# Half-width products in the inverse of a chunked recurrence

## The chip, the cores and the metric

The kernel runs on one core of a Trainium2 chip. The metric is the device time of one execution in microseconds (us), and shorter is better. The engines are called PE (matrix products; PEld is its weight load), VectorE (DVE in the rows), ScalarE (ACT), GpSimd (POOL) and SyncE (SP).

## The reference

One layer of a hybrid decoder for 2048 tokens of width 1024, in float32. After a norm, one projection feeds two groups: differential attention, and the RWKV-7 recurrence of 8 heads of width 64. Their outputs go through an output projection; a mixture of 32 experts and a gated per-layer embedding follow. What matters here is the recurrence:

```python
def step(state, inp):
    r_t, w_t, k_t, v_t, a_t, b_t = inp
    sa = jnp.einsum('bhvk,bhk->bhv', state, a_t)
    state = (state * w_t[:, :, None, :] + sa[..., None] * b_t[:, :, None, :]
             + v_t[..., None] * k_t[:, :, None, :])
    y = jnp.einsum('bhvk,bhk->bhv', state, r_t)
    return state, y
```

## The kernel before

The kernel is a row of phases, one after the other with a barrier between them: constants, projection, attention, the recurrence (`phase_rwkv`), output projection, routing, experts and the final gate. All the work in question is in `phase_rwkv`.

The recurrence is computed in chunks of 64 tokens (`CK`). A tile has 128 tokens, so two chunks (`CHUNKS`: partitions 0 to 63 and 64 to 127), and there are 16 tiles. Within a chunk the step-by-step update needs the inverse of a triangular 64 by 64 matrix for each head. It is built up by doubling. `T` holds the inverse of the diagonal blocks found so far. Level 0 fills `T` directly from the product `G3`. Each level l from 1 to 5 then does this, for 8 heads and 2 chunks:

- `Tr(l-1)`: four transposes of `T` on PE; ScalarE copies them to `TP` (128x512).
- `X(l)a` and `X(l)b`: products of `AR1` with `T`, one job for each chunk. ScalarE copies each to `X` (128x256).
- `TX(l)a` and `TX(l)b`: products of `TP` with `X`, one job for the even heads and one for the odd. VectorE copies each into `T` by `copy_predicated` under the mask `lv` of the level (`fill_T`, 128x256).

At level l the mask of an entry is set where row and column lie in neighbouring blocks of 2^l, the row's block being the odd one. So only columns in the first half of each block pair of 2^(l+1) can be set: 32 of the 64.

All products here are of float32. The program's `nc.tensor.matmul` appears in the trace as two weight loads and two matmuls, so a job of X or TX, which has 8 products, counts 16 matmuls; with 20 such jobs a tile that makes 320. Weights are 64x64, and the moving operand has 64 columns. A 64x64 weight takes a quarter of the array. An X job reads one half of the partitions and writes both halves, so it alternates between two quarters; so does a TX job.

The engines take their work in fixed orders written out by hand (`PE_JOBS`, `ACT_EV`, `DVE_EV`, `POOL_EV`), each with one counting semaphore. A PE job waits at its start, never in its middle. Between the steps of a level stands other work: after `X1` the job `Wa`, after `TX1` `Wb`; after `X2` `MN0` and `MN1` (L1618 to L1620), and nothing between `TX2b` and `Tr2`; after `X3` `S0`, `RT0` and `RT1` (L1624), after `TX3` `Y0` (L1628, L1630), `S1`, `Ya` and `Yb`; after `X4` `pc` (L1573), after `TX4` `T0` (L1647); after `X5` `T1` and `D` (L1642), after `TX5` `T2` and `T3`, then `Tr5`, and `cum`, `G3`, `G1`, `G2` of the next tile. W, MN, S, RT, Y0 and Y belong to the tile before ("tail"); cum, pc and T0 to T3 prepare the next one ("prep"). Tile 0 has no tail work and the last tile has no prep. PE's program is unrolled over the tiles; the other engines run a loop.

The waits on which the steps of a level hang:

```python
job(f"Tr{level}", make, (DV, "G3b" if level == 0 else f"TX{level}b", 0))
...
     (DV, "G1b" if level == 1 else f"TX{level - 1}b", 0))
...
job(f"TX{level}{f}", make, (AC, f"X{level}b", 0), (AC, f"Tr{level - 1}", 0))
```

Of the kernel before, what the change touches and what calls it, by code (L numbers as in the profile page):

```python
# [14 lines left out]
P = 128  # L15
# [985 lines left out]
HV = 8  # L1001
CK = 64
# [46 lines left out]
def bank_of(name):  # L1049
    return MAIN_JOBS.index(name) % BANKS if name in MAIN_JOBS else BANKS + PREP_JOBS.index(name) % 2  # L1050
# [11 lines left out]
def phase_rwkv(nc, t, ident):  # L1062
# [5 lines left out]
    with ExitStack() as ctx:  # L1068
        sb = lambda n, s, d=F32: ctx.enter_context(nc.sbuf_tensor(n, s, d))
        sem = lambda n: t["semctx"].enter_context(nc.semaphore(n))  # L1070
        two = lambda n, s, d=F32: [sb(f"{n}{k}", s, d) for k in range(2)]
# [10 lines left out]
        pc = two("c_pc", [P, 4, 2])  # L1082
        AR1 = two("c_AR1", [P, HV, 2, CK]); AR2 = two("c_AR2", [P, HV, 2, CK])
        T = two("c_T", [P, HV, CK])
        TT = two("c_TT", [P, HV, CK]); TP = sb("c_TP", [P, 4, 2, CK]); X = sb("c_X", [P, 2, 4, CK])
        WU = sb("c_WU", [P, HV, 2, DH]); RpT = sb("c_RpT", [P, 4, P]); Y0 = sb("c_Y0", [P, RW])
        MT = sb("c_MT", [P, 2, 4, DH]); NN = sb("c_NN", [P, 2, 4, DH]); St = sb("c_Stmp", [P, 4, DH])
        S = [two(f"c_S{k}", [P, 4, DH]) for k in range(2)]
# [3 lines left out]
        lv = sb("c_levels", [P, len(LEVELS), CK], I32); bits = sb("c_bits", [P, 3, CK], I32)  # L1092
# [8 lines left out]
        def bank(name):  # L1101

            return ps[:, bank_of(name), :]
# [6 lines left out]
        def steps(eng, body):  # L1110

            body(-1, 1, {"prep"}, None)
            body(0, 0, {"main", "prep"}, None)
            with eng.Fori(0, (TILES - 2) // 2) as j:
                body(j * 2 + 1, 1, {"main", "tail", "prep"}, j)
                body(j * 2 + 2, 0, {"main", "tail", "prep"}, j)
            body(TILES - 1, 1, {"main", "tail"}, None)
            body(TILES, 0, {"tail"}, None)
# [5 lines left out]
        def group(name):  # L1124
            return "tail" if name in TAIL else "prep" if name in PREP else "main"

        def heads(ap):
            return ap.rearrange("p (h d) -> p h d", d=DH)

        @block.sync  # L1130
        def _(sp):
# [172 lines left out]
        @block.scalar  # L1304
        def _(act):
            act.wait_ge(cs_p, 1)

            def step(i, s, what, j):
                n = 1 - s

                def ev(name, make, *waits):
                    if group(name) in what:
                        for e, other in waits:
                            act.wait_ge(e.sem, e.value(other, i))
                        AC.in_order(name)
                        make().then_inc(AC.sem, 1)
                    else:
                        AC.in_order(name)
                        act.drain().then_inc(AC.sem, 1)

                def evac(name, out, src=None, waits=()):

                    b = bank(name)
                    ev(name, lambda: nc.scalar.copy(out, src(b) if src else b), (PE, name), *waits)

                def four(b):
                    return b.rearrange("p (h n) -> p h n", h=4)

                def narrow(b):
                    return b[:, 0:4 * CK].rearrange("p (h n) -> p h n", h=4)  # L1330

                def tr(level):
                    evac(f"Tr{level}", TP[:].rearrange("p j c n -> p (j c n)"))

                def w_(f):
                    evac(f"W{f}", WU[:, half(f), :, :].rearrange("p h a d -> p h (a d)"), four)

                def x_(level, f):
                    evac(f"X{level}{f}", X[:, AB.index(f), :, :], narrow)
                def t_(p):  # L1340
                    evac(f"T{p}", cT[n][:, p, :, :], lambda b: b.rearrange("p (k n) -> p k n", k=4), ((DV, "RT1"),))
                tr(0)
                x_(1, "a")
                x_(1, "b")
                w_("a")
                w_("b")
                tr(1)
                if "prep" in what:
                    act.wait_ge(PE.sem, PE.value("cum", i))
                    act.wait_ge(PO.sem, PO.value("Kh", i - 1)) if not (isinstance(i, int) and i < 0) else None  # L1350
                    act.wait_ge(DV.sem, DV.value("Bh", i - 1)) if not (isinstance(i, int) and i < 0) else None
                    nc.scalar.activation(Pt[:], bank("cum"), ACT.Exp, scale=-DECAY)
                ev("P", lambda: nc.scalar.activation(iP[:], bank("cum"), ACT.Exp, scale=DECAY))
                ev("cumsb", lambda: nc.scalar.copy(cumsb[:], bank("cum")))
                x_(2, "a")
                x_(2, "b")
                ev("sqk", lambda: nc.scalar.activation(sq[:], kk0[:], ACT.Square), (PO, "kk0"))
                tr(2)
                x_(3, "a")
                x_(3, "b")  # L1360
                evac("Y0", Y0[:])
                ev("Pex", lambda: nc.scalar.activation(Pex[:], cumsb[:], ACT.Exp, scale=-DECAY), (PO, "ex"))
                tr(3)
                x_(4, "a")
                x_(4, "b")
                ev("pc", lambda: nc.scalar.activation(pc[n][:], bank("pc")[:, 0:8].rearrange("p (a c) -> p a c", c=2), ACT.Exp, scale=-DECAY),
                   (PE, "pc"), (DV, "S1"))
                tr(4)
                ev("sqy", lambda: nc.scalar.activation(sq[:], y[:], ACT.Square), (DV, "yc"))
                x_(5, "a")  # L1370
                x_(5, "b")
                for p in range(4):
                    t_(p)
                evac("Tr5", TT[s][:], lambda b: b.rearrange("p (h n) -> p h n", h=HV))
                ev("vcopy", lambda: nc.scalar.copy(V[n][:], rkv[n][:, 2 * RW:3 * RW]), (PO, "rkv"), (PE, "Y0"))
                evac("D", AD[s][:, 1, :, :], heads)
            steps(act, step)

        @block.vector
        def _(dve):  # L1380
# [16 lines left out]
            def step(i, s, what, j):  # L1397
                n = 1 - s
# [14 lines left out]
                def fill_T(name, level, f):  # L1413

                    def make():
                        src = bank(name)[:, 0:4 * CK].rearrange("p (h n) -> p h n", h=4)
                        m = lv[:, level, :].unsqueeze(1).broadcast_to([P, 4, CK])
                        return nc.vector.copy_predicated(T[s][:, half(f), :], m, src)  # L1418
                    ev(name, make, (PE, name))

                def masked(name, dst, f):
# [78 lines left out]
        def _(pe):  # L1500
            pe.wait_ge(cs_p, 1)

            def step(i, s, what, j):
                n = 1 - s
# [23 lines left out]
                def job(name, make, *waits):  # L1528
                    if not skipped(name):
                        ready((name,), waits)  # L1530
                        PE.in_order(name)
                        make(bank(name)).then_inc(PE.sem, 1)
# [14 lines left out]
                def each(name, hs, mm, *waits):  # L1547
                    def make(b):
                        for h in hs:
                            last = mm(b, h)  # L1550
                        return last
                    job(name, make, *waits)
# [9 lines left out]
                def cols(b, h, w):  # L1562
                    return b[:, h * w:(h + 1) * w]

                def at(h):
                    return slice(DH * (h % 2), DH * (h % 2) + DH)
# [31 lines left out]

                def x_(level, f):
                    r = CHUNKS[AB.index(f)]  # L1600
                    each(f"X{level}{f}", range(HV), lambda b, h: nc.tensor.matmul(cols(b[at(h)], h // 2, CK), AR1[s][r, h, 0, :], T[s][r, h, :], start=True, stop=True),
                         (DV, "G1b" if level == 1 else f"TX{level - 1}b", 0))

                def tx(level, f):
                    def make(b):
                        for h in hs_of(f):
                            for c, r in enumerate(CHUNKS):
                                last = nc.tensor.matmul(cols(b[r], h // 2, CK), TP[at(h), h // 2, c, :], X[at(h), c, h // 2, :], start=True, stop=True)  # L1608
                        return last
                    job(f"TX{level}{f}", make, (AC, f"X{level}b", 0), (AC, f"Tr{level - 1}", 0))  # L1610

                def w_(f):
                    chunked(f"W{f}", hs_of(f), lambda b, h, r: nc.tensor.matmul(cols(b, h // 2, P), TT[n][r, h, :], AD[n][r, :, h, :], start=True, stop=True),
                            (AC, "D", 1))
# [39 lines left out]
                def level(l):  # L1654
                    tr(l - 1); x_(l, "a"); x_(l, "b")
# [19 lines left out]
def half(f):  # L1675
    return slice(AB.index(f), HV, 2)


def hs_of(f):
    return range(AB.index(f), HV, 2)  # L1680
# [1168 lines left out]
```

## Time and profile before

| | |
|---|---|
| time, median of 3 runs | 3408.14 us (3404.29 to 3421.78) |
| time of the profiled execution | 3406.95 us |
| its span, first to last instruction | 3405.3 us |
| mean granted clock of PE | 0.946 |
| PE busy | 3016.2 us (89%) |
| PE weight loads busy | 2430.4 us (71%) |
| VectorE busy | 2080.1 us (61%) |
| ScalarE busy | 1572.2 us (46%) |
| GpSimd busy | 793.8 us (23%) |

The profiled execution takes 1.65 us more than its span and lies 1.2 us under the median. PE's busy time is that of modelled, overlapping matmuls, so a high share does not say that PE could not be faster.

### The profile page before, as it was taken

Reading aid. Unit: us, or ns where it says so; the run is one execution under the profiler, and the core shown is the slowest. Engines: PE = TensorE matmul, PEld = TensorE weight load, DVE = VectorE, ACT = ScalarE, POOL = GpSimd, SP = SyncE. Lnnn points to the kernel's source line nnn. Section 1 sums busy time; section 2 is a strip of 40 time slices with the busy share of each in tenths; the row PEclk is TensorE's granted clock in tenths of the full one; section 3 lists DMA queues with packets and bytes.
Section 4 is the critical chain, followed back from the end, with each engine's and each line's share of the span. In section 5 each row is a group of like instructions: output and inputs, shape, how many; then the busy total and the mean of one; then the engine's idle time right before and its main releaser. Section 6 shows DMA issues by size and latency. Waiting matters only on the chain. (4 is left out here: it accounts for less than half of the span.)

```text
span 3405.3 us, 69237 instructions
## 1 busy us (share of the span) xinstructions
PE 3016.2 (89%) x25224; PEld 2430.4 (71%) x25224; DVE 2080.1 (61%) x3031; ACT 1572.2 (46%) x2560; POOL 793.8 (23%) x1065
## 2 busy tenths in 40 slices
PE   7999999996899857888887799299999999995899
PEld 5776887884666636777776688278787787874787
DVE  4443772224778754566564333689798888985565
ACT  3332211004778743434343211078787787875232
POOL 1000330001123144666664000000000100001343
PEclk9999999998999977999999899599999999997999
DMA  5555347556000021222220665536968777673343
GB/s 171 182 189 195 125 160 255 196 186 176 7 10 14 7 81 52 77 83 72 82 71 18 233 211 196 215 125 238 350 261 328 285 281 295 261 303 144 124 145 110
DMA packets 246700, 554.37 MB, mean 163 GB/s; under 512 B 28032, under 2 KB 64000, under 8 KB 238240
## 3 DMA queue, kind: packets, MB, share of 16 engines
q1 hardware_dynamic: 228112, 484.07, 40.3%
q0 software_dynamic: 11552, 41.95, 3.4%
q10 hardware_dynamic: 6768, 24.64, 1.8%
q8 instruction: 183, 3.00, 0.3%
q14 instruction: 85, 0.70, 0.1%
HBM read 408.52 MB, written 142.09 MB: 162 GB/s over the span
## 5 line engine op out<-in xcount | busy, mean ns | idle before, releaser
L583 PE MATMUL p_z<-w_in_part,hn_split 128*128 128x512 f32 x2304 | 536.4, 393 | 9.1 <-DMA hn_split<-s_hT 4.7
L583 PEld LDWEIGHTS p_z<-w_in_part,hn_split 128*128 128x128 f32 x2304 | 433.7, 189 | 99.9 <-DMA hn_split<-s_hT 5.5
L1739 DVE TENSOR_TENSOR e_w_part<-w_gate_up_sb,e_w_part 128x1024 fp32r<-128x1024 f32 x380 | 453.1, 1221 | 58.3 <-ACT e_w_part L1734 56.9
L1734 ACT CAST e_w_part<-w_gate_up_sb 128x1024 fp32r x380 | 397.3, 1053 | 160.7 <-PE pe_gate L2500 73.6
L2500 PE MATMUL pe_gate<-e_w_part,e_xT 128*128 128x512 f32 x1128 | 287.1, 412 | 26.2 <-DVE e_w_part L1739 26.2
L2512 PE MATMUL pe_y<-e_w_part,e_hT 128*128 128x512 f32 x1128 | 276.3, 401 | 13.2 <-DVE e_w_part L1739 13.2
L2500 PEld LDWEIGHTS pe_gate<-e_w_part,e_xT 128*128 128x128 f32 x1128 | 218.0, 197 | 77.8 <-issue 21.3
L2500 PE MATMUL pe_up<-e_w_part,e_xT 128*128 128x512 f32 x1128 | 271.0, 396 | 0.0
L1739 DVE TENSOR_TENSOR e_w_part<-w_down_sb,e_w_part 128x1024 fp32r<-128x1024 f32 x188 | 218.0, 1219 | 62.0 <-ACT e_w_part L1734 61.8
L2512 PEld LDWEIGHTS pe_y<-e_w_part,e_hT 128*128 128x128 f32 x1128 | 209.9, 189 | 60.7 <-DVE e_w_part L1739 13.6
L2500 PEld LDWEIGHTS pe_up<-e_w_part,e_xT 128*128 128x128 f32 x1128 | 211.9, 188 | 51.3
L2301 POOL COPY e_idx<-row_tokens 128x1 uint32<-128x1 uint32 (+1 forms) x48 | 26.5, 551 | 816.5 <-PE pe_xT L2477 572.3
L1746 PE MATMUL pd_out<-d_w_out_part,d_mixT 128*128 128x512 f32 x768 | 188.3, 401 | 11.6 <-DVE d_w_out_part L1739 11.6
L1734 ACT CAST e_w_part<-w_down_sb 128x1024 fp32r x188 | 188.3, 1055 | 16.0 <-PE pe_up L2500 14.6
L943 PE MATMUL p_scores<-kT_all,qT_all 64*128 64x512 f32 (+3 forms) x768 | 176.3, 514 | 16.6 <-DVE ident_half L851 16.3
L800 ACT ACTIVATE prob<-p_scores,neg_max 128x640 f32<-128x640 f32 (+5 forms) x240 | 176.6, 743 | 19.7 <-DVE neg_max L872 13.2
L1746 PE MATMUL pf_gate<-f_w_gate,f_hgT 128*128 128x512 f32 x768 | 179.0, 393 | 2.4 <-DVE f_hgT L1739 2.4
L1746 PEld LDWEIGHTS pd_out<-d_w_out_part,d_mixT 128*128 128x128 f32 x768 | 143.8, 191 | 43.8 <-issue 11.9
L1418 DVE COPY_PREDICATED c_T<-c_levels,p_ring 128x256 f32<-128x256 int32 x192 | 76.6, 441 | 156.4 <-PE p_ring L1608 112.4
L1746 PEld LDWEIGHTS pf_gate<-f_w_gate,f_hgT 128*128 128x128 f32 x768 | 145.7, 190 | 33.2 <-DVE f_hgT L1739 2.8
L985 PE MATMUL p_o<-v_all,attnT 128*128 128x128 f32 x1088 | 150.8, 278 | 8.3 <-issue 6.8
L985 PEld LDWEIGHTS p_o<-v_all,attnT 128*128 128x128 f32 x1088 | 136.1, 194 | 11.5 <-issue 11.3
(424 smaller groups left out, 5590.9 us busy)
## 6 DMA issues: line engine op xcount, KB each, us to landing
w_gate_up_sb<-in_w_gate_dram SPq DMA_DIRECT2D x32, 2048.0 KB, 13.1
w_gate_up_sb<-in_w_up_dram SPq DMA_DIRECT2D x32, 2048.0 KB, 19.4
w_down_sb<-in_w_down_dram SPq DMA_DIRECT2D x32, 2048.0 KB, 9.2
hn_split<-s_hT SPq DMA_DIRECT2D x48, 1024.0 KB, 5.0
s_y<-e_y ACTq DMA_DIRECT2D x47, 512.0 KB
s_hT<-hn_split SPq DMA_DIRECT2D x16, 1024.0 KB, 6.5
s_y<-d_zeros SPq DMA_DIRECT2D x16, 1024.0 KB, 6.4
s_zn<-z_stage SPq DMA_DIRECT2D x48, 256.0 KB, 2.0
```

The source lines that it names most:

```text
L583: last = nc.tensor.matmul(bank, hs[m % 3][:, a, k, :].bitcast(F32R), w_part(c, b)[:, k, :].bitcast(F32R), start=(k == 0 and a == b == 0), ...
L800: nc.scalar.activation(prob[g % 2][m][:, EDGE[g][c]:EDGE[g][c + 1]], scores_of(n, W[g][c])[:, m, :], ACT.Exp, bias=nmax[g % 2][:, c, m:m + ...
L943: return nc.tensor.matmul(out[:, m, a:b], qT[r, h, ROW[g], :], kT[r, h, k0:k0 + (b - a) // P, :], start=True, stop=stop)
L985: last = nc.tensor.matmul(pO[:], aT[n % 2][:, b * P:(b + 1) * P], v[:, HEAD[g], kb, :], start=(kb == 0), stop=(kb == ROW[g]))
L1418: return nc.vector.copy_predicated(T[s][:, half(f), :], m, src)
L1734: return nc.scalar.copy(high, src)
L1739: return nc.vector.tensor_tensor(low, src, high, ALU.subtract)
L1746: last = nc.tensor.matmul(out, lhsT(a, k), rhs(b, k), start=(start and k == 0 and n == 0), stop=(stop and k == steps - 1 and n == len(PART ...
L2301: pool.tensor_copy(idx[:], ids[:, bass.ds(i, 1)]).then_inc(idx_ready, 1)
L2500: last = nc.tensor.matmul(bank[:], xT[a][:, g % 4 * 2 + k, :], ring[b][:, g % 4, k * DX:(k + 1) * DX], start=first, stop=final)
L2512: last = nc.tensor.matmul(p_y[:, half, :], hT[a][:, g, :], ring[b][:, g, half * BANK:(half + 1) * BANK], start=first, stop=final)
```

## The change

From level 1 on, X and TX take only the 32 columns that the mask can set, through a strided view of `T` (`first_halves`): m runs of 2^l columns, every second block. The result of X lies packed in PSUM and in a buffer `X` of half the size; TX takes it packed. The copies of `X` on ScalarE shrink from 128x256 to 128x128, and the fills on VectorE from 128x256 to 128x128, with a strided view of `T` and of the mask. The number of instructions, their order, the waits, the weights and level 0 stay as they are.

```diff
-        TT = two("c_TT", [P, HV, CK]); TP = sb("c_TP", [P, 4, 2, CK]); X = sb("c_X", [P, 2, 4, CK])
+        TT = two("c_TT", [P, HV, CK]); TP = sb("c_TP", [P, 4, 2, CK]); X = sb("c_X", [P, 2, 4, CK // 2])
...
+        def first_halves(ap, level):
+            if len(ap.shape) == 2:
+                return ap.rearrange("p (m two b) -> p m two b", two=2, b=2 ** level)[:, :, 0, :]
+            return ap.rearrange("p h (m two b) -> p h m two b", two=2, b=2 ** level)[:, :, :, 0, :]
...
                 def narrow(b):
-                    return b[:, 0:4 * CK].rearrange("p (h n) -> p h n", h=4)
+                    return b[:, 0:2 * CK].rearrange("p (h n) -> p h n", h=4)
...
                 def fill_T(name, level, f):
 
                     def make():
-                        src = bank(name)[:, 0:4 * CK].rearrange("p (h n) -> p h n", h=4)
-                        m = lv[:, level, :].unsqueeze(1).broadcast_to([P, 4, CK])
-                        return nc.vector.copy_predicated(T[s][:, half(f), :], m, src)
+                        if level == 0:
+                            src = bank(name)[:, 0:4 * CK].rearrange("p (h n) -> p h n", h=4)
+                            m = lv[:, level, :].unsqueeze(1).broadcast_to([P, 4, CK])
+                            return nc.vector.copy_predicated(T[s][:, half(f), :], m, src)
+                        src = bank(name)[:, 0:2 * CK].rearrange("p (h m b) -> p h m b", h=4, b=2 ** level)
+                        m = first_halves(lv[:, level, :], level).unsqueeze(1).broadcast_to([P, 4, CK // 2 ** (level + 1), 2 ** level])
+                        return nc.vector.copy_predicated(first_halves(T[s][:, half(f), :], level), m, src)
...
                 def x_(level, f):
                     r = CHUNKS[AB.index(f)]
-                    each(f"X{level}{f}", range(HV), lambda b, h: nc.tensor.matmul(cols(b[at(h)], h // 2, CK), AR1[s][r, h, 0, :], T[s][r, h, :], start=True, stop=True),
+                    each(f"X{level}{f}", range(HV), lambda b, h: nc.tensor.matmul(cols(b[at(h)], h // 2, CK // 2).rearrange("p (m b) -> p m b", b=2 ** level), AR1[s][r, h, 0, :], first_halves(T[s][r, h, :], level), start=True, stop=True),
...
-                                last = nc.tensor.matmul(cols(b[r], h // 2, CK), TP[at(h), h // 2, c, :], X[at(h), c, h // 2, :], start=True, stop=True)
+                                last = nc.tensor.matmul(cols(b[r], h // 2, CK // 2), TP[at(h), h // 2, c, :], X[at(h), c, h // 2, :], start=True, stop=True)
```

## Rows read from the trace of the kernel before

**Rows 1.** The page: span, PE's busy tenths and granted clock in 40 slices.

```profile
span 3405.3 us, 69237 instructions
...
PE   7999999996899857888887799299999999995899
...
PEclk9999999998999977999999899599999999997999
```

**Rows 2.** Busy time and granted clock (PEclk) in stretches of the recurrence's stage.

```profile
core 0: us, PE busy (x) PEld busy (x) DVE busy (x) ACT busy (x) POOL busy (x), PEclk, DMA share, GB/s
1284.00:1325.00 41.00, 34.28 (x524) 28.48 (x524) 14.06 (x24) 14.03 (x30) 18.67 (x16) 0.61 0.19 53
...
1325.50:1782.60 457.10, 399.02 (x10588) 353.77 (x10584) 276.56 (x533) 192.13 (x416) 295.07 (x252) 0.96 0.25 77
...
1557.00:1562.00 5.00, 4.66 (x123) 4.66 (x125) 2.72 (x6) 0.40 (x1) 2.03 (x4) 0.66 0.27 91
```

**Rows 3.** Groups by line, 1325 to 1850 us: busy, mean ns, idle before.

```profile
L1608 PE MATMUL p_ring<-c_X,c_TP 64*64 64x64 f32 x2400 | 80.3, 230 | 11.5 <-issue 10.9 <-ACTq L1319 0.6
L1601 PE MATMUL p_ring<-c_T,c_AR 64*64 64x64 f32 x2400 | 77.5, 228 | 2.6 <-issue 2.3
L1418 DVE COPY_PREDICATED c_T<-c_levels,p_ring 128x256 f32<-128x256 int32 x180 | 71.6, 441 | 132.7 <-PE p_ring L1608 97.8 <-PE p_ring L1582 33.4 <-issue 0.4
...
L1324 ACT COPY c_X<-p_ring 128x256 f32<-128x256 f32 x150 | 50.5, 381 | 5.4 <-PE p_ring L1601 2.6
```

**Rows 4.** Timeline of PE in one tile, 1519 to 1532 us: start, length, what.

```profile
1519.66 0.63 PE L1595 MATMUL p_ring<-ident,c_T 128*128 128x128 f32 x4 [0.75 <-issue]
1520.22 0.97 PE L1601 MATMUL p_ring<-c_T,c_AR 64*64 64x64 f32 x32
...
1528.46 1.05 PE L1573 MATMUL p_ring<-c_ind,c_sig 128*128 128x2 f32 x8
1529.44 1.05 PE L1608 MATMUL p_ring<-c_X,c_TP 64*64 64x64 f32 x32
...
1531.25 0.63 PE L1595 MATMUL p_ring<-ident,c_T 128*128 128x128 f32 x4 [0.16 <-DVE c_T L1418]
```

**Rows 5.** Waits of PE, 1325 to 1830 us: total, times, longest.

```profile
PE p_ring L1608 <- issue: 10.9, 10, 3.1
...
PE p_ring L1628 <- issue: 9.2, 5, 2.8
PE p_ring L1618 <- issue: 9.1, 5, 2.3
```

**Rows 6.** The timeline of rows 4 elsewhere: two array quarters at work, and four.

```profile
1500.78 1.15 PE L1642 MATMUL p_ring<-c_V,c_AR 64*64 64x64 f32 x32
...
1521.66 0.57 PE L1624 MATMUL p_ring<-c_AR,c_WU 64*64 64x64 f32 x25
```

**Rows 7.** Timeline of PE in the output projection: 36 columns.

```profile
1921.64 1.87 PE L1944 MATMUL pd_logits<-d_w_router,d_h2T 128*128 128x36 f32 x16
```

**Rows 8.** Timeline of PE in the attention stage: 128 columns.

```profile
1012.09 1.13 PE L985 MATMUL p_o<-v_all,attnT 128*128 128x128 f32 x8
```

**Rows 9.** Timeline of VectorE, the two fills of level 2.

```profile
1518.79 0.78 DVE L1418 COPY_PREDICATED c_T<-c_levels,p_ring 128x256 f32<-128x256 int32 x2 [0.94 <-PE p_ring L1608]
```

**Rows 10.** VectorE, an operation of 128 columns, over the whole span.

```profile
L2053 DVE TENSOR_TENSOR r_masked<-r_masked,r_group_off 128x128 f32<-128x128 f32 x4 | 0.9, 286 | 0.1
```

**Rows 11.** ScalarE by shape over the whole span.

```profile
L1324 ACT COPY c_TP<-p_ring 128x512 f32<-128x512 f32 x80 | 46.9, 586 | 170.0 <-PE p_ring L1595 169.9
...
L821 ACT COPY attnT<-p_attnT 128x128 f32<-128x128 f32 x16 | 4.1, 257 | 2.8 <-PE p_attnT L973 2.7
```

**Rows 12.** Timeline of PE in the last tile, without the next tile's work.

```profile
1840.03 0.97 PE L1608 MATMUL p_ring<-c_X,c_TP 64*64 64x64 f32 x32 [0.56 <-ACTq L1319]
1841.78 0.63 PE L1595 MATMUL p_ring<-ident,c_T 128*128 128x128 f32 x4 [0.77 <-DVE c_T L1418]
```

## The prediction

> **What bounds the kernel now.** I read the page first. The span is 3405.3 us [rows 1]. The phases run one after the other, so what the recurrence's stage gains or loses shows in full at the end. The stage fills about slices 15 to 22 of 40; PE is 80 to 90% busy there, and its granted clock is mostly 9 tenths [rows 1]. Next I read the stretches. From 1325.5 to 1782.6 us there are 13 tiles, 35.2 us each. PE is busy for 399.0 of 457.1 us, VectorE for 276.6, GpSimd for 295.1, ScalarE for 192.1 [rows 2]. PE bounds the stage, then, but 58.1 us, or 4.5 us a tile, are not its work.
>
> I looked for those 4.5 us in the waits. Most stand as "issue" before L1608, L1618 and L1628: 29.2 us in 20 waits in 505 us [rows 5]. They cannot be waits for data, because L1618 and L1628 wait inside a job, where the program has no wait. They come after dense runs of small matmuls, and I take them for late delivery of PE's unrolled program. The change leaves every instruction in place, so it neither removes nor moves them. A wait that hangs on the change stands once in each tile before the transposes after `TX2b`: 0.75 us, where no other job lies between [rows 4]. A shorter one, 0.16 us, stands before the transposes after `T0` [rows 4]. Here PE waits for the second fill.
>
> **Part 1: the matmuls.** 320 matmuls a tile go from 64 to 32 moving columns. X and TX are PE's largest groups in the stage: 77.5 and 80.3 us busy over 15 tiles, 228 and 230 ns each [rows 3]. But these lengths overlap; what counts is the step from one start to the next. In job D 32 such matmuls alternate between two quarters and span 1.15 us [rows 6]. Less the last one's own 0.23 us, that is 0.92 us for 15 further steps of a quarter: 61 ns. With four quarters at work, 25 matmuls span 0.57 us [rows 6], (0.57 - 0.23) / 24 = 14 ns each and so 57 ns for a quarter. Does this step come from 64 moving columns or from the 64 columns of the weight? This kernel has no 64-column weight with fewer moving columns, but they have three widths behind a 128-column weight. With 2 columns, 8 matmuls span 1.05 us: (1.05 - 0.25) / 7 = 114 ns [rows 4]. With 36 columns, 16 span 1.87 us: (1.87 - 0.28) / 15 = 106 ns [rows 7]. With 128 columns, 8 span 1.13 us: (1.13 - 0.28) / 7 = 121 ns [rows 8]. Two columns cost as much as 128. The step follows the weight there, and half of 114 ns is 57 ns, just what a quarter takes now. I conclude that a 64-column weight holds the step at 57 to 61 ns for 32 moving columns as for 64. Value taken: nothing saved. The other bound is a step of half the length: 320 x 14 ns = 4.5 us a tile, 72 us in 16 tiles.
>
> The Trainium skill has a rule for each outcome. "TensorE: Matmul & The Clock Gate", section "LDWEIGHTS (loading the stationary operand)", says that a weight load takes its column count divided by 1.2 ns, whatever the rows; as an estimate 53 ns for 64 columns, by which this sum saves nothing. "TensorEngine Tiling (Array Packing)", section "Instruction Overhead", gives each matmul a floor of some 60 cycles, below which fewer columns gain nothing; at 2.4 GHz that is an estimated 25 ns, by which the step would halve and the stage gain most of the 72 us. The trace's 114 ns for two columns speaks for the first.
>
> **Part 2: the tail of a job.** A job's last matmul ends sooner. Half the columns can save at most half of a quarter's 57 ns step, some 25 ns, on each handover to ScalarE or VectorE. I take 25 ns, with 0 as the other bound.
>
> **Part 3: the fills.** A fill of 128x256 takes 441 ns [rows 3]. Two of them span 0.78 us, so the second starts 0.34 us after the first [rows 9]. The nearest row with 128 columns is 286 ns [rows 10]; 441 - 286 = 155 ns. It doesn't read PSUM through a mask, so I take 135 ns. Views with runs of 2 to 32 elements under a mask occur nowhere in the trace. At worst I let them cost twice the 286 ns, 572 ns, which is 131 ns more than now.
>
> **Part 4: the copies of X.** 381 ns for 256 columns [rows 3], 586 ns for 512, 257 ns for 128 [rows 11]: 124 ns off the mean, 205 / 2 = 103 by slope. I take 100 ns. In steady tiles this is hidden: PE works on Wa, MN, S and RT, pc, or T1 and D between X and TX, and no wait of TX for ScalarE is long enough to be listed. Without that cover it is worth 100 ns a level.
>
> **The sum.** In the 14 middle tiles PE waits for the second fill at two places. Each gets shorter by 135 + 25 = 160 ns: the first fill already ends before the second product does. The 0.16 us after T0 goes entirely, the 0.75 us becomes 0.59. Per tile 0.32 us, in 14 tiles 4.5 us. Of this I keep two thirds, 3 us, because a PE that arrives earlier at the next dense run may wait longer there for its program. The first and the last tile lack half of the covering jobs. In the last one PE waits 0.56 us before TX and 0.77 us before the transposes [rows 12]. There a level can gain 100 + 25 before TX and 160 before Tr, 0.29 us; for 5 levels in 2 tiles that is 2.9 us, and I take 2 because some levels keep cover. Total: -5 us. From the profiled execution's 3406.95 us this gives 3402 us. It lies 1.2 us under the median of 3408.14 us, a difference too small to carry. I forecast 3402 us. A difference below 0.5% (17 us) can hardly be told from none here.
>
> The likeliest case has its own bounds. With every gain kept (0.32 x 16 plus 2.9 for the ends, -8) and some program waits shifting in our favour it gives 3392 us. With the worst fills both of a level's fills are late, 4 x 131 ns in 16 tiles, +8 us, and 3416 us.
>
> **Rivals.**
> - *The step halves with the columns.* The step of 57 to 61 ns would be explained equally well by the 64 moving columns, since weight and moving width are equal there. Against it stand 114 ns for two columns [rows 4]. It would free 4.5 us a tile. Cover is thinner then, and denser runs wait more for the program; I let it keep half to all, 36 to 72 us: 3335 to 3371 us, middle 3352 us. Chance 0.16.
> - *PE's clock falls more often.* Between 1557 and 1562 us the granted clock is 0.66, so of these 5 us 3.4 were at 1.2 GHz, right after a wait of PE; over the 13 tiles it is 0.96, so 8%, or 37 us, at the lower level [rows 2], and these cost about 18 us. Before 1325 us, with thin work, it is 0.61 [rows 2]. If halved moving columns count as less activity, the clock will fall again in each tile. A fall of 3.4 us costs 1.7 us, so one more in each of 16 tiles is +27 us less the 5 above: 3429 us. It decides (over 17 us) from 13 further falls on. Against it: the weight loads remain as dense, and the falls now follow long waits. Chance 0.08.
> - *The fills become slow* through short runs: +8 us at most as worked out, which stays within 0.5%; it is a part of the likeliest case.
>
> **How the numbers follow.** The likeliest case, 0.74, lies wholly within 0.5%. The halved step, 0.16, is faster by over 0.5%; the clock, 0.08, slower. The last 0.02 I split. That makes faster 0.17, same 0.74, slower 0.09. The likeliest case alone holds less than 8 in 10, so the range reaches into both others: down to 3358 us, the slower third of the first rival, and up to 3422 us, the milder half of the second.
>
> **What would show it.** After the change, the groups of X and TX should have 64x32 matmuls, each about 25 ns shorter, but jobs of 32 that still span 0.9 us or more; a job of about 0.5 us would prove me wrong. The fills should be near 305 ns, the copies near 280 ns. PE's wait before the transposes after TX2b should be near 0.6 us and the one after T0 gone. Tiles should follow each other every 35 us. The waits inside MN and Y0 should remain. The mean clock between 1325 and 1782 us should stay near 0.96; if it fell below 0.9 the second rival would be at work. I would be wrong above all if a weight of 64x64 loads faster than half of a 128x128 one.

## The result, and the profile after

The change made the kernel slower, by less than half a per cent: 3428.11 us (median of 8 runs, 3416.89 to 3447.70) against 3415.43 us (median of 8, 3404.29 to 3422.14), ratio 1.0044, 95% interval 1.0026 to 1.0063. I had forecast 3402 us and a range up to 3422 us. The forecast started from 3406.95 us, the profiled execution of the kernel before, which lies 8 us under the median of its 8 runs. As a difference, I forecast a gain of 5 us and the medians show a loss of 13.

The page of the profiled execution after the change, which took 3416.89 us; the same lines as [rows 1]:

```profile
span 3415.2 us, 69237 instructions
...
PE   7999999996899858899998699399999999995899
...
PEclk9999999998999977889888899599999999997999
```

The span is 9.9 us longer than in [rows 1]. PE's busy tenths look the same or fuller. The granted clock does not: where it read 9 in slices 17 to 22, it now reads mostly 8.

Busy time and granted clock (PEclk) after the change: up to the second tile, the 13 middle tiles, the end, and the whole stage with a few microseconds of its neighbours:

```profile
core 0: us, PE busy (x) PEld busy (x) DVE busy (x) ACT busy (x) POOL busy (x), PEclk, DMA share, GB/s
1250.00:1325.30 75.30, 39.90 (x552) 32.56 (x552) 27.21 (x58) 16.42 (x36) 40.27 (x50) 0.55 0.33 109
1325.30:1791.10 465.80, 423.47 (x10587) 378.55 (x10583) 264.70 (x533) 182.65 (x416) 294.91 (x253) 0.87 0.25 75
1791.10:1876.00 84.90, 71.79 (x1892) 65.42 (x1890) 38.00 (x84) 26.12 (x59) 35.21 (x32) 0.86 0.06 19
1250.00:1876.00 626.00, 535.17 (x13024) 476.52 (x13024) 329.91 (x675) 225.18 (x511) 370.39 (x334) 0.83 0.23 72
```

The 13 middle tiles of [rows 2] took 457.1 us at a clock of 0.96 and now take 465.8 us at 0.87. PE is busy for 423.5 us of them, 24 us more than before, though it streams fewer columns. PE's idle time in these tiles fell from 58.1 to 42.3 us, so a part of what the lower clock costs went into waits that were there anyway. VectorE (264.7 against 276.6) and ScalarE (182.7 against 192.1) have less to do, as intended. The last of these windows is fixed in time, and the stage ends at 1875.8 us here and at 1861.5 us in the kernel before. From the first to the last matmul of the stage the kernel after and the kernel before give:

```profile
1264.60:1875.80 611.20, 535.17 (x13024) 476.51 (x13024) 325.04 (x648) 225.18 (x511) 366.86 (x313) 0.84 0.22 67
...
1264.50:1861.50 597.00, 503.46 (x13024) 443.88 (x13024) 340.99 (x648) 237.17 (x511) 368.80 (x313) 0.92 0.22 68
```

Groups by line between 1325 and 1850 us, after; they answer to [rows 3]:

```profile
L1617 PE MATMUL p_ring<-c_X,c_TP 64*64 64x32 f32 x2368 | 81.5, 235 | 7.5 <-issue 7.0 <-ACTq L1324 0.5
L1610 PE MATMUL p_ring<-c_T,c_AR 64*64 64x32 f32 x2370 | 79.4, 237 | 4.0 <-issue 3.7
...
L1427 DVE COPY_PREDICATED c_T<-c_levels,p_ring 128x128 f32<-128x128 int32 x148 | 44.5, 327 | 124.0 <-PE p_ring L1617 122.6 <-issue 0.3
...
L1329 ACT COPY c_X<-p_ring 128x128 f32<-128x128 f32 x148 | 37.9, 274 | 10.0 <-PE p_ring L1610 7.7
```

The fills went from 441 to 327 ns in the mean (median 296), the copies of X from 381 to 274 ns. The matmuls, with half the columns, did not get shorter. The numbers behind `x2560` are the shortest, the median and the longest in ns, for X before and after:

```profile
L1601 PE MATMUL p_ring<-c_T,c_AR x2560: 212/218/367, 1296.0 to 1843.1; 64*64 64x64 f32 x197
...
L1610 PE MATMUL p_ring<-c_T,c_AR x2560: 186/219/313, 1294.3 to 1850.6; 64*64 64x32 f32 x197
```

The median is 219 ns where it was 218, so I had the 25 ns wrong by which each was to be shorter. The means, 235 and 237 ns where they were 230 and 228, rose because more of the matmuls ran at the lower clock.

Where did the clock fall? The timeline of PE after the change, levels 4 and 5 of one tile:

```profile
1492.88 0.92 PE L1610 MATMUL p_ring<-c_T,c_AR 64*64 64x32 f32 x32
...
1494.71 0.92 PE L1617 MATMUL p_ring<-c_X,c_TP 64*64 64x32 f32 x32
...
1497.26 1.53 PE L1610 MATMUL p_ring<-c_T,c_AR 64*64 64x32 f32 x32
...
1499.76 1.86 PE L1651 MATMUL p_ring<-c_V,c_AR 64*64 64x64 f32 x29
```

And the busy time of each engine, with the granted clock, in two stretches there:

```profile
1490.00:1495.00 5.00, 5.00 (x112) 4.66 (x110) 2.72 (x6) 2.33 (x6) 1.98 (x2) 0.76 0.10 18
1495.80:1502.80 7.00, 7.00 (x108) 6.11 (x106) 2.63 (x7) 2.69 (x6) 2.05 (x3) 0.51 0.16 42
```

In the kernel before, the same two levels of the same tile ran at the full clock:

```profile
1495.00:1502.00 7.00, 6.80 (x159) 5.96 (x159) 5.75 (x11) 3.58 (x10) 0.73 (x2) 1.00 0.30 80
```

After the change PE is busy for 5.00 of 5.00 us from 1490 to 1495 us, and the clock comes back up from an earlier fall. Right after that, from 1495.8 to 1502.8 us, it is busy for 7.00 of 7.00 us at a granted clock of 0.51, so at 1.2 GHz nearly throughout. Just ahead of it stands no wait, only `Tr3`, X4, pc, TX4 and the first of T0; of these X4 and TX4 have 32 moving columns and pc has 2. A pair of X jobs takes 1.53 us there against 0.92 us just before; job D, which the change does not touch, takes 1.86 us for 29 of its matmuls. In the kernel before, the same job takes 1.15 us [rows 6].

The transposes after `TX2b` and after `T0` in the tile of [rows 4], by the timeline of PE after the change:

```profile
1519.94 0.63 PE L1604 MATMUL p_ring<-ident,c_T 128*128 128x128 f32 x4 [0.56 <-issue]
...
1531.99 0.63 PE L1604 MATMUL p_ring<-ident,c_T 128*128 128x128 f32 x4
```

The first wait shrank from 0.75 to 0.56 us, and the second, of 0.16 us, is gone. Over the whole kernel PE's idle time before these transposes (behind the bar: busy, mean ns, then idle) went from 16.7 to 11.2 us, near the 5 us of my sum:

```profile
L1595 PE MATMUL p_ring<-ident,c_T 128*128 128x128 f32 x320 | 54.8, 296 | 16.7 <-issue 12.3 <-DVE c_T L1418 3.8
...
L1604 PE MATMUL p_ring<-ident,c_T 128*128 128x128 f32 x320 | 58.3, 311 | 11.2 <-issue 9.2 <-DVE c_T L1427 1.9
```

The waits of PE between 1325 and 1830 us, after:

```profile
PE p_ring L1604 <- issue: 8.1, 14, 0.9
PE p_ring L1627 <- issue: 7.7, 4, 2.3
PE p_ring L1637 <- issue: 7.4, 4, 2.2
PE p_ring L1617 <- issue: 7.0, 7, 2.3
```

The waits inside MN and Y0 (L1627, L1637) are still there, a little shorter than in [rows 5]. Those before the transposes (L1604) are 8.1 us; before the change they were:

```profile
PE p_ring L1595 <- issue: 10.9, 15, 1.1
```

No new wait of any size has come in. PE is busy for longer and idle for less, and what made it busy for longer is its clock.

### The profile page after: what moved, and what is told of

Same layout as the page of the kernel before. It is cut to its first block and busy times, and to the rows that moved or that the text cites. A ratio compares the mean times of both kernels' runs of the same rounds, so it can differ in the third digit from the quotient of the medians.

```text
span 3415.2 us, 69237 instructions
## 1 busy us (share of the span) xinstructions
PE 3044.9 (89%) x25224; PEld 2461.6 (72%) x25224; DVE 2063.8 (60%) x3031; ACT 1561.7 (46%) x2560; POOL 794.3 (23%) x1065
## 5 line engine op out<-in xcount | busy, mean ns | idle before, releaser
L943 PE MATMUL p_scores<-kT_all,qT_all 64*128 64x512 f32 (+3 forms) x768 | 176.0, 513 | 16.1 <-DVE ident_half L851 15.8
L1427 DVE COPY_PREDICATED c_T<-c_levels,p_ring 128x128 f32<-128x128 int32 x160 | 48.0, 327 | 140.4 <-PE p_ring L1617 138.7
```

What stands on the lines that cost most here:

```text
L943: return nc.tensor.matmul(out[:, m, a:b], qT[r, h, ROW[g], :], kT[r, h, k0:k0 + (b - a) // P, :], start=True, stop=stop)
L1427: return nc.vector.copy_predicated(first_halves(T[s][:, half(f), :], level), m, src)
```

## The experiments

My theory after the result: the clock follows the columns that PE streams, and the half-width products made it fall, while the smaller copies and fills did gain what they promised. The rivals are that the strided views, on PE or elsewhere, cost the time, or that the smaller work of ScalarE and VectorE left PE idle more often and that lowered the clock.

**Full stream, half copies and fills (`x64_t64`).** X reads all 64 columns of `T`, the useful halves first; the copy takes these; TX reads the packed 32 columns twice. The edits of the copy's and the fill's view are left out here.

```diff
-nc.tensor.matmul(cols(b[at(h)], h // 2, CK // 2).rearrange("p (m b) -> p m b", b=2 ** level), AR1[s][r, h, 0, :], first_halves(T[s][r, h, :], level), start=True, stop=True)
+nc.tensor.matmul(cols(b[at(h)], h // 2, CK).rearrange("p (two m b) -> p two m b", two=2, b=2 ** level), AR1[s][r, h, 0, :], T[s][r, h, :].rearrange("p (m two b) -> p two m b", two=2, b=2 ** level), start=True, stop=True)
...
-nc.tensor.matmul(cols(b[r], h // 2, CK // 2), TP[at(h), h // 2, c, :], X[at(h), c, h // 2, :], start=True, stop=True)
+nc.tensor.matmul(cols(b[r], h // 2, CK).rearrange("p (two n) -> p two n", two=2), TP[at(h), h // 2, c, :], X[at(h), c, h // 2, :].unsqueeze(1).broadcast_to([CK, 2, CK // 2]), start=True, stop=True)
```

> PE streams 64 columns again in X and TX (X reads T as its first block halves and then the others, a strided view of all 64; TX reads the packed 32 columns twice), while the copies of X and the fills stay at half size. If the narrow moving operand lowers the clock, the time falls below the kernel before, by the 3 to 8 us that the smaller fills and copies give: ratio to before 0.997 to 1.000, and the mean granted clock of the middle 13 tiles near 0.96, not 0.87. If strided views or the half-size copies are to blame, the ratio stays near 1.004 and the clock near 0.87.

Measured: 3396.33 us, ratio to before 0.9951 (0.9932 to 0.9970), so 17 us faster than before, where I expected 3 to 8, and 32 us faster than after the change. From the kernel after it differs in the streamed columns, and in that copies and fills skip the unused half in PSUM. Windows of `x64_t64`, middle tiles and stage:

```profile
1321.90:1773.50 451.60, 399.39 (x10584) 354.99 (x10582) 268.04 (x533) 180.89 (x416) 297.03 (x252) 0.94 0.25 78
...
1262.40:1849.90 587.50, 502.18 (x13024) 444.13 (x13024) 329.51 (x648) 223.16 (x511) 370.76 (x313) 0.92 0.23 69
```

The clock of the middle tiles is back at 0.94, that of the stage at 0.92, as before the change, against 0.84 after it. Every run has its clock over the whole kernel on record, which is firmer than one profile. The median is 0.946 in 6 runs of `x64_t64`, 0.943 in the 23 runs of the kernel before beside it, and 0.931 in 8 runs after the change, and the highest after the change (0.933) is below the lowest of the other two (0.940). This kernel keeps the strided views, the short copies and the short fills, so they did not make the clock fall.

**Half the dose: only TX narrow (`x64_t32`), only X narrow (`x32_t64`).** Each takes one of the two edits above.

> Only TX takes 32 columns; X streams 64. If the clock follows the columns streamed, this is half of the dose: clock of the middle tiles between 0.89 and 0.94, ratio to before 1.000 to 1.003. If the strided reading of T in X is to blame, it stays as after the change, since X still reads T strided: 1.004.

> Only X takes 32 columns; TX streams 64. By the columns streamed it is the same half dose as with the narrow TX: clock 0.89 to 0.94, ratio 1.000 to 1.003. If it matters which job is narrow (the one that stands before the sparse pc and transposes of level 4), the two halves differ clearly.

Measured: 3417.15 us, ratio 1.0008 (0.9994 to 1.0022), and 3417.30 us, ratio 1.0010 (0.9998 to 1.0022). Both lie between 0.9951 and 1.0044, and it does not matter which of the two is narrow. The median clock over the whole kernel is 0.936 in both, between 0.946 and 0.931. The stage of `x64_t32`:

```profile
1268.40:1878.90 610.50, 526.28 (x13024) 466.69 (x13024) 322.53 (x648) 225.13 (x511) 367.04 (x313) 0.86 0.22 67
```

and of `x32_t64`:

```profile
1266.30:1863.00 596.70, 510.23 (x13024) 451.13 (x13024) 332.23 (x648) 223.86 (x511) 370.05 (x313) 0.89 0.22 68
```

0.86 and 0.89 lie between 0.92 and 0.84. For the middle tiles alone they read 0.89 and 0.94, the two ends of what I expected. A single profile scatters; the medians of 12 and 11 runs are the firmer evidence.

**Contiguous instead of strided (`contig32`).** X multiplies the first 32 columns of `T`, side by side. The kernel so computes another product, and its results are other numbers.

```diff
-nc.tensor.matmul(cols(b[at(h)], h // 2, CK // 2).rearrange("p (m b) -> p m b", b=2 ** level), AR1[s][r, h, 0, :], first_halves(T[s][r, h, :], level), start=True, stop=True)
+nc.tensor.matmul(cols(b[at(h)], h // 2, CK // 2), AR1[s][r, h, 0, :], T[s][r, h, 0:CK // 2], start=True, stop=True)
```

> X multiplies the first 32 columns of T, contiguous, in place of the 32 that the mask can set: that part of the computation is changed, all sizes and the order are those after the change. If the width lowers the clock, nothing changes against the kernel after: ratio to before about 1.004, clock of the middle tiles about 0.87. If strided reading on PE costs time or clock, it returns to before, 1.000 or less.

Measured: 3434.60 us, ratio 1.0069 (1.0049 to 1.0089), overlapping the 1.0026 to 1.0063 after the change. Its middle tiles and its stage:

```profile
1325.10:1791.50 466.40, 423.32 (x10585) 379.52 (x10583) 262.74 (x533) 181.98 (x416) 293.93 (x252) 0.86 0.25 75
...
1266.00:1876.60 610.60, 533.58 (x13024) 476.10 (x13024) 323.51 (x648) 224.35 (x511) 367.50 (x313) 0.84 0.22 67
```

The clock is 0.86, and the stage takes 610.6 us at 0.84 where it takes 611.2 us at 0.84 after the change. The narrow stream does it, strided or not. What `contig32` takes beyond the kernel after lies elsewhere. Its other numbers route the tokens otherwise, and the experts' stage, which runs as many blocks as the routing needs, has 84 matmuls more and is 13.5 us longer; the kernel after, then `contig32`:

```profile
2221.80:3134.40 912.60, 866.27 (x3956) 703.07 (x3956) 777.44 (x710) 714.14 (x757) 79.86 (x94) 0.98 0.70 266
...
2222.60:3148.70 926.10, 884.31 (x4040) 717.86 (x4040) 794.58 (x725) 728.74 (x773) 80.34 (x96) 0.98 0.69 263
```

**A quarter (`x16_t32`).** X multiplies 16 columns and the copy writes them twice (the copy's edit is not shown). Half of the needed product is left out.

```diff
+nc.tensor.matmul(cols(b[at(h)], h // 2, CK // 2)[:, 0:CK // 4], AR1[s][r, h, 0, :], T[s][r, h, 0:CK // 4], start=True, stop=True)
```

> X multiplies only the first 16 columns of T (half of the needed product is left out, and the copy writes the 16 columns twice), so that X streams a quarter of the columns before; TX as after the change, copies and fills as after. If the columns streamed set the clock, it falls below the 0.83 that the whole stage has after the change, and the time rises by another 5 to 15 us: ratio 1.006 to 1.011. If the clock only follows PE's idle time, it stays at 1.004 and 0.83, as the step is held by the weights.

Measured: 3444.70 us, ratio 1.0094 (1.0070 to 1.0119). Its middle tiles, its stage and its experts' stage:

```profile
1324.90:1795.80 470.90, 428.55 (x10586) 385.05 (x10583) 261.31 (x533) 182.29 (x416) 295.04 (x253) 0.85 0.25 74
...
1264.90:1880.80 615.90, 538.21 (x13024) 481.09 (x13024) 321.60 (x648) 224.70 (x511) 366.58 (x313) 0.83 0.22 66
...
2226.70:3152.60 925.90, 884.11 (x4040) 717.90 (x4040) 794.37 (x725) 728.70 (x773) 80.02 (x96) 0.98 0.69 263
```

The ratio lies where I expected it, but mostly by luck: the experts' stage is 13.3 us longer, from other numbers as in `contig32`. The stage takes 4.7 us more than after the change, and the middle tiles go from 465.8 to 470.9 us and from 0.87 to 0.85. That points the expected way and is less than single profiles scatter, so it is not shown that a quarter costs more than a half. It did not gain anything.

**Only the fills (`fill_half`), only the copies (`copy_half`)**, both with 64 columns streamed.

> Only the fills shrink; PE streams 64 columns and the copies of X are 128x256. The kernel with both at half size was 0.9951 of before, more than the 0.998 that my sum for fills and copies gives. If the fills carry it, because PE waits for the second fill in every tile, this gives 0.995 to 0.998. If the copies carry it, it is 0.998 or above.

> Only the copies of X shrink to 128x128; PE streams 64 columns, the fills are 128x256. By my sum the copies are covered in the middle tiles and open only in the first and last: 1 us, ratio 0.999 to 1.000. If they are worth as much as the fills, 0.997 to 0.998.

Measured: fills 3402.20 us, ratio 0.9956 (0.9939 to 0.9973); copies 3404.83 us, ratio 0.9977 (0.9959 to 0.9995). The fills are worth 15 us (9 to 21), not the 5 or so of my sum. The copies gave 8 us by the ratio where I expected 1, with an interval that reaches from 2 to 14 us. The intervals overlap, so it is not shown that the fills carry more. Both kernels, and `x64_t64`, also stream `T` in X in another order, useful halves first. No run has this order alone, so a part of all three gains may come from it.

**Four quarters at work (`quads_before`, `quads_x64`, `quads_x32`).** The step of a quarter looks to be held by its weight, and X and TX keep only two quarters busy. These kernels interleave the a and b jobs matmul by matmul with the program's own `two_jobs`; the first on the kernel before, the second on `x64_t64`, the third with 32 columns streamed.

```diff
+def xs(level):
+    def make(b, k, n_):
+        r = CHUNKS[k]
+        return nc.tensor.matmul(cols(b[at(n_)], n_ // 2, CK), AR1[s][r, n_, 0, :], T[s][r, n_, :], start=True, stop=True)
+    two_jobs((f"X{level}a", f"X{level}b"), make, (DV, "G1b" if level == 1 else f"TX{level - 1}b", 0))
...
+def filled(level):
+    def make(b, k, n_):
+        c, h = n_ % 2, 2 * (n_ // 2) + k
+        r = CHUNKS[c]
+        return nc.tensor.matmul(cols(b[r], h // 2, CK), TP[at(h), h // 2, c, :], X[at(h), c, h // 2, :], start=True, stop=True)
+    two_jobs((f"TX{level}a", f"TX{level}b"), make, (AC, f"X{level}b", 0), (AC, f"Tr{level - 1}", 0))
```

> The kernel before at full width, with the a and b jobs of X interleaved matmul by matmul, and those of TX, so that four quarters of the array work at once. If a weight of 64 columns holds a quarter for 57 ns, the step of a matmul falls from 24 to 30 ns to about 14 and a job pair of 32 from 0.97 us to about 0.65; 0.3 us saved ten times a tile, 48 us in all, of which waits for the program and the fills take back a part, and the clock may fall. 15 to 45 us faster than before: ratio 0.987 to 0.996. If the delivery of the program or the clock takes all of it back, 1.000 or above.

> The same interleaving, with 64 columns streamed and half-size copies of X and fills. With thinner PE work the second fill and the copies lie open in more places, so their 0.1 to 0.16 us should now be worth more than in the kernel that only streams 64: 5 to 15 us below the interleaved kernel before, ratio 0.983 to 0.994. If the clock falls because PE is idle more often, the gain stays below 5 us.

> The interleaved kernel with 32 columns streamed, which differs from the interleaved one with 64 only in this. If the weights hold a quarter for 57 ns in this order too, the narrower stream gives no time back and costs clock: 15 to 35 us slower than the interleaved one with 64, ratio 0.993 to 1.000. If with four quarters at work the moving columns were the limit, it would be faster than 0.989.

Measured: 3390.78 us, ratio 0.9929 (0.9911 to 0.9946); 3376.41 us, ratio 0.9890 (0.9872 to 0.9909); 3383.27 us, ratio 0.9909 (0.9885 to 0.9933). The timeline of PE in `quads_x64`, a pair of X jobs:

```profile
1332.00 0.69 PE L1611 MATMUL p_ring<-c_T,c_AR 64*64 64x64 f32 x32
```

and in `quads_x32`:

```profile
1345.84 0.67 PE L1611 MATMUL p_ring<-c_T,c_AR 64*64 64x32 f32 x32
```

32 matmuls take 0.69 us from the first start to the last end, where the kernel before took 0.97 [rows 4], and 0.67 us with half the columns. With four quarters too, halving the columns buys no more than 0.02 us for 32 matmuls. The middle tiles of `quads_x64`:

```profile
1324.00:1748.90 424.90, 368.90 (x10587) 322.40 (x10582) 274.48 (x533) 176.97 (x416) 299.03 (x252) 0.96 0.27 82
```

and of `quads_x32`:

```profile
1321.10:1753.80 432.70, 384.51 (x10586) 338.88 (x10583) 273.19 (x533) 177.19 (x416) 298.65 (x253) 0.90 0.27 81
```

0.96 and 424.9 us against 0.90 and 432.7 us: the narrow stream costs clock here as well, and time by this pair of profiles. Over the whole kernel every run of `quads_x32` (0.937 to 0.942) has a lower clock than every run of `quads_x64` (0.943 to 0.947). The medians differ by 7 us, though, less than the 15 to 35 I expected, and the intervals overlap, so that the loss in time is not shown for this order. `quads_x64` is faster than the kernel before by 1.1% and than the kernel after by more. It saves less than its shorter jobs: 0.28 us ten times a tile would be 45 us in 16 tiles, and the interleaving brought 23 us on the kernel before. Part of the rest went into PE's wait before the transposes. Between 1325 and 1750 us it is 6.8 us in `x64_t64`, and with the interleaving, in `quads_x64`:

```profile
PE p_ring L1604 <- issue: 16.0, 13, 2.0
```

**Narrower weights (`x_w32`).** The kernel after, each product of X cut in two with weights of 32 columns.

```diff
+for q in range(2):
+    o = slice(DH * (h % 2) + 32 * q, DH * (h % 2) + 32 * q + 32)
+    last = nc.tensor.matmul(cols(b[o], h // 2, CK // 2).rearrange("p (m b) -> p m b", b=2 ** level), AR1[s][r, h, 0, 32 * q:32 * q + 32], first_halves(T[s][r, h, :], level), start=True, stop=True)
```

> The kernel after, with each product of X cut into two with weights of 32 columns (output rows 0 to 31 and 32 to 63 of a head), 32 moving columns each: 64 matmuls for a pair of X jobs in place of 32. If the weight's columns hold the step, a 32-column weight holds its part of the array for 28 to 30 ns, and four parts work at once: 7 to 8 ns a matmul, 0.5 us for a pair of jobs at the full clock, against 0.7 us from first to last start now. If instead every matmul holds its part for some 57 ns whatever its weight, it is 14 ns a matmul and 0.9 us. The whole kernel need not be faster, as PE's program is a fifth longer.

Measured: 3431.63 us, ratio 1.0036 (1.0022 to 1.0051), no better as a whole. Two X jobs in its timeline:

```profile
1360.14 0.79 PE L1615 MATMUL p_ring<-c_T,c_AR 64*32 64x32 f32 x64
...
1364.08 0.76 PE L1615 MATMUL p_ring<-c_T,c_AR 64*32 64x32 f32 x64
```

64 matmuls take 0.76 us; less the last one's 0.19 us, that is 0.57 us from first to last start, near the 0.5 that I expected from the weight's width and far from the 0.9 of a fixed price. (0.76 - 0.19) / 63 = 9 ns each, and with four parts of the array at work 36 ns for each part, the change from one job to the other included. With weights of 64 columns and the same 32 moving columns, `quads_x32` gives (0.67 - 0.22) / 31 = 14.5 ns and 58 ns for a part, about the 57 ns of 64 moving columns by [rows 6]. So the step falls with the width of the weight, if not quite by half. The middle tiles became longer all the same (475.5 us at a clock of 0.91), with 160 more matmuls and as many more weight loads a tile.

## Why the prediction was wrong

**The step of the matmuls: right.** I held that a weight of 64 columns keeps a quarter for 57 to 61 ns whatever it streams, from three widths behind a 128-column weight. A pair of jobs, 32 matmuls with 32 columns, takes 0.92 us against 0.97 us. The end of a job does come some 0.05 us sooner, but not for the reason of my part 2, a shorter last matmul: the median one takes 219 ns against 218. `x_w32` keeps the moving columns and halves the weight's width, and the step of a part falls to 36 ns. The rival of a halved step, 0.16, is refuted. By the Trainium skill, "TensorE: Matmul & The Clock Gate", section "LDWEIGHTS (loading the stationary operand)", the time of a weight load is in proportion to the weight's columns. The traces agree in that the step grows with them, 36, 57 and 114 ns for 32, 64 and 128, though the first is more than half of the second.

**Fills and copies: the wait that I costed was right, the whole gain was not.** A fill fell by 114 ns in the mean and by about 145 ns in the median, a copy by 107 ns, near the 135 and 100 ns taken. PE's wait before the transposes after `TX2b` shrank by 0.19 us, where I had 0.16, and the one after `T0` went, as forecast. Over the whole kernel PE's idle time before the transposes fell by 5.5 us after the change and by 5.4 us in `x64_t64` (16.7 to 11.3), which is the 5 us of my sum. But with the stream held at 64 columns the gain in time is 17 us (10 to 23), more than the 8 of my bound. What the other 12 or so are is not settled: the order in which X streams `T` was changed with it, and the profile of one execution can't tell, because such profiles scatter by as much (the one of `fill_half` took 3411.19 us, 9 us over its median).

**The clock: here the prediction failed.** The step was the second rival: "If halved moving columns count as less activity, the clock will fall again in each tile." I priced it at one more fall of 3.4 us a tile, 27 us, and gave it 0.08, on the ground that "the weight loads remain as dense, and the falls now follow long waits". The first ground was wrong, and the second described the kernel before and did not carry over. Dense weight loads did not keep the clock up: PE was busy for 12.00 of 12.00 us in the two stretches shown, its weight loads for 4.66 of 5.00 and 6.11 of 7.00, and the clock was at 1.2 GHz in the second. The measured price is 32 us: `x64_t64` against the kernel after. That it lies near my 27 is in part luck. By the mean clocks of the 13 middle tiles, 0.96 and 0.87, I estimate 37 us at the lower level before and 121 us after. That is 84 us more, where my one fall a tile makes 54 us in 16 tiles, and half of 84 would be 42 us in these tiles alone. The waits took a part of it: PE's busy time rose by 24.5 us and its idle time fell by 15.8. With the 17 us of the smaller copies and fills taken off, that leaves 15; the two medians differ by 13. So the likeliest case combined a gain of 5 with a loss of 0, and measured were a gain of 17 and a loss of 32. The starting point adds to the miss of 26 us: 8 us of it are the 3406.95 us from which I counted. Since the time moved less than 17 us in the end, it stays within what I called no difference, but above the top of my range.

The profile of before offered something that I did not use. The clock stood at 0.96 in the middle tiles with falls inside the stage (0.66 from 1557 to 1562 us [rows 2]), so it wasn't safe there. By my own sum PE would save no time by streaming less, so all that the narrower stream could do to PE's time was to cost clock. That made the balance of risks one-sided.

## What to carry to other kernels

Before narrowing a moving operand, find what holds the step of the matmul: if it is the weight, fewer columns gain next to nothing and may cost clock, as they did here. Take the smaller size where it pays, in copies and fills, and try letting PE stream the full width, even columns that nobody reads: that was 32 us faster here. To shorten such a product, put more quarters of the array to work at once: it gained 23 us here, where narrowing lost. And when an experiment leaves out a part of the computation, look at the other stages too: here other numbers made the experts' stage 13 us longer.

## What the runs showed of the hardware

- In these kernels the granted clock fell with the moving columns, with PE's instructions, weights and order unchanged. With 64 columns in X and TX, with one of the two at 32, and with both at 32, the median clock over the whole kernel is 0.946, 0.936 and 0.931 and the ratio to before 0.9951, 1.0008 and 1.0010, 1.0044, with the copies and fills at half size in all of them. PE can be busy for 7.00 of 7.00 us at a clock of 0.51.
- Three widths of a float32 weight, three steps of one part of the array: 36 ns with 32 columns, 57 ns with 64, 114 ns with 128, at the full clock. 2, 36 or 128 moving columns make little difference to the last (114, 106 and 121 ns), and 32 or 64 little to the second: 0.67 against 0.69 us for 32 matmuls on four quarters.
- The fill's mask and destination in runs of 2 to 32 elements cost next to nothing extra: 296 ns in the median for 128x128, where a plain operation of that size takes 286 ns [rows 10].
